# Sliding-window attention of a decoder trunk: heads interleaved in the small products, a tile's value product moved into a later unit, and the tail of the stage reordered

## The chip, the cores and the metric

One Trainium2 core runs the whole kernel. The metric is the device time of one execution in microseconds. 
## The reference

One inference step of a two-layer decoder over 512 prompt positions and 8 sample sequences of 8 positions each (576 columns, 1024 features). Layer 0 is half a SwiGLU, a state-space mixer, half a SwiGLU. Keys and values are projected once. Layer 1 is half a SwiGLU, the attention below, half a SwiGLU. Only the attention is touched here:

```python
def sink_alibi_attention(q, k, v, dist, valid, sinks):
    s = jnp.einsum('...qkgd,...skd->...kgqs', q, k).astype(jnp.float32) * (ATT_HEAD_DIM ** -0.5)
    s = s - alibi_slopes()[:, :, None, None] * dist
    s = jnp.where(valid, s, -jnp.inf)
    ...
    p = jax.nn.softmax(jnp.concatenate([s, sink_col], axis=-1), axis=-1)[..., :-1]
    return jnp.einsum('...kgqs,...skd->...qkgd', p.astype(v.dtype), v)
```

There are 16 query heads of 64 features on 4 key/value heads and a window of 128. A block of 128 prompt queries sees its own 128 keys and the 128 before. A sample sequence sees 128 cached keys and its own 8 new ones. The result goes through the output projection `o @ attn_w_o` and is added to the residual stream.

## The kernel before

The program is written engine by engine: five instruction lists (PE, ACT, DVE, POOL, SP) with hand-placed semaphore waits, each list run strictly in order. Nothing is scheduled by a planner.

**Weights.** They come in units of 128 output features by 1024 input features. SP loads a unit into `wraw` (two buffers), ACT rounds it to a high part (`split_hi`, L887 to L891), DVE subtracts to get the low part (`split_lo`, L1300 to L1303). A unit on PE (`unit`, L400; `half_unit`, L422) is 8 input tiles by three products (high weight with high and low data, low weight with high data) by two column halves of 288: 48 products. Unit n+2 can only be split when unit n has been multiplied, because they share a buffer.

**Attention loop.** `attention` of PE (L783) runs 8 units `j`; each yields the queries of two heads (`h` = 0 and 1, in partitions 0 to 63 and 64 to 127). For unit j the lists hold:

- PE (L786 to L799): the unit's 48 products; the 14 transposes of the probabilities of unit j-1 (`turn_probs`, L761); the scores of unit j, all of head 0, then all of head 1 (`scores`, L746, 8 matrix instructions a head); the value product of unit j-1, head 0, then head 1 (`weigh_values`, L772, 28 instructions).
- DVE (L1729 to L1743): queries out of PSUM (`qs`), `split_lo` of unit j+2, softmax input of both heads (`softmax_in`, four instructions a head), denominators, low part of the output of unit j-1 (`out_lo`).
- ACT (L1207 to L1227): `split_hi` of unit j+2, the sample queries (L1220), copies of the two transposed heads (`copy_probs`), exponentials of both heads, high part of the output of unit j-1 (`out_hi`).
- POOL (L1947): scales the probabilities of each head by the reciprocal denominators.

A matrix product of plain f32 operands is two matrix instructions in the trace; a transpose, and a product of the rounded (fp32r) operands, is one.

**Tail.** After the loop PE computes the sample scores (`sample_scores`, L810, 64 instructions of 136 columns), waits for the probabilities of unit 7, turns and weighs them, turns the sample probabilities (L827, L829), runs a quarter of the first two output tiles (`half_tile`, L835), then the sample values (L852 to L858): for each of 8 sequences and 2 pairs of heads one product with the cached values and one with the 8 new values, 64 instructions of 64 columns. The new values `Vnew` come back from HBM through a POOL DMA (L1957). The other three quarters of the two output tiles follow, and then `residual("o", ...)`, the remaining six output tiles.

## Time and profile before

| | |
|---|---|
| median of 3 runs | 2482.21 us (2475.89 to 2486.93) |
| profiled execution, its own time | 2485.29 us |
| its span, first to last instruction | 2483.7 us |
| mean granted TensorE clock | 0.986 |
| attention, first score product to the first product of the third output tile | 1845.8 to 2004.1 us |

The page gives each engine's busy time, forty slices of the span, and the chain of work that ended last. Times inside the span are counted from its start. "PEld" is TensorE's weight load, which runs beside the products. A PE that is busy need not be at its peak, because ends of products are modelled. The granted clock is given as a share of full speed (1.00 is 2.4 GHz, 0.50 is 1.2 GHz).

### The profile page before, as it was taken

The page shows a single profiled execution, that of the slowest core. Times are in us where ns is not written, and L with a number is a line of the kernel's source. Part 1 is how long each engine was busy: PE and PEld are TensorE (multiplying, and loading weights), DVE is VectorE, ACT ScalarE, POOL GpSimd, SP SyncE. Part 2 cuts the span into 40 slices and gives each one's busy share as a digit, 9 for nine tenths or more (in the row PEclk, how much of TensorE's full clock was granted, in tenths as well). Part 3 has the DMA queues.
Part 4 walks back from the last instruction along what each step waited for, and adds up shares of the span by engine and source line. Part 5 has one row for each costly group of instructions (what it writes and reads, how often), then busy time and mean ns, then how long its engine had stood idle before and what let it go on. Part 6 is the DMA issues. An engine that isn't in the chain of part 4 may idle for free.

```text
span 2483.7 us, 45807 instructions
## 1 busy us (share of the span) xinstructions
PE 2415.9 (97%) x18177; PEld 2365.4 (95%) x18177; DVE 1205.9 (49%) x1475; ACT 845.0 (34%) x1336; POOL 326.6 (13%) x278
## 2 busy tenths in 40 slices
PE   8999999899999999999999999999999999999997
PEld 8999999889888899999999999999989899999997
DVE  5344333778899934443433444343346354344323
ACT  4222222456666522222222322222235423222212
POOL 0000011322333221000012000000222140000021
PEclk9999999999999999999999999999999899999999
DMA  3222222335555322222222222222231022222222
GB/s 131 83 84 80 80 93 85 121 120 180 173 176 178 130 77 85 81 80 84 84 85 93 77 79 81 84 84 86 90 108 41 18 68 76 84 84 78 84 92 80
DMA packets 66239, 234.92 MB, mean 95 GB/s; under 512 B 7920, under 2 KB 8048, under 8 KB 66016
## 3 DMA queue, kind: packets, MB, share of 16 engines
q1 hardware_dynamic: 52560, 187.72, 22.3%
q0 software_dynamic: 8368, 31.59, 3.9%
q10 hardware_dynamic: 5248, 14.76, 1.8%
q8 instruction: 41, 0.67, 0.1%
q14 instruction: 22, 0.18, 0.0%
HBM read 221.37 MB, written 14.64 MB: 95 GB/s over the span
## 4 chain that ended last, share of the span: by engine, by line
PE 90%; DVE 5%; issue 2%; ACT 1%; DMA 1%; ACTq 0%; POOL 0%; DVEq 0%; POOLq 0%
PE psum L412 75%; PE psum L430 6%; DVE cacc L1418 1%; PE psum L757 1%; PE psum L707 1%; DVE wlo L1302 1%; PE psum L484 1%; DMA E<-decay_rows 1%; PE psum L768 1%; PE psum L603 1%; PE psum L598 1%; PE psum L780 1%; PE psum L840 0%; DVE grs L1654 0%; PE psum L633 0%
## 5 line engine op out<-in xcount | busy, mean ns | idle before, releaser
L1302 DVE TENSOR_TENSOR wlo<-wraw,whi 128x1024 fp32r<-128x1024 f32 x342 | 436.7, 1277 | 982.5 <-ACT whi L891 982.5
L891 ACT ACTIVATE whi<-wraw 128x1024 fp32r<-128x1024 f32 x349 | 369.4, 1059 | 946.8 <-PE psum L412 919.6
L412 PE MATMUL psum<-xhi,whi 128*128 128x288 f32 x3120 | 672.6, 297 | 11.4 <-POOL wlo L1969 7.3
L412 PE MATMUL psum<-xlo,whi 128*128 128x288 f32 x3120 | 669.5, 296 | 0.0
L412 PE MATMUL psum<-xhi,wlo 128*128 128x288 f32 x3120 | 669.5, 296 | 0.0
L412 PEld LDWEIGHTS psum<-xhi,whi 128*128 128x128 f32 x3120 | 504.7, 189 | 15.1 <-issue 14.4
L412 PEld LDWEIGHTS psum<-xlo,whi 128*128 128x128 f32 x3120 | 504.5, 189 | 0.0
L412 PEld LDWEIGHTS psum<-xhi,wlo 128*128 128x128 f32 x3120 | 504.3, 189 | 0.0
L412 PE MATMUL psum<-hhi,whi 128*128 128x288 f32 x1408 | 302.7, 296 | 0.0
L412 PE MATMUL psum<-hhi,wlo 128*128 128x288 f32 x1408 | 302.6, 296 | 0.0
L412 PE MATMUL psum<-hlo,whi 128*128 128x288 f32 x1408 | 302.6, 296 | 0.0
L412 PEld LDWEIGHTS psum<-hhi,wlo 128*128 128x128 f32 x1408 | 226.5, 189 | 0.0
L412 PEld LDWEIGHTS psum<-hhi,whi 128*128 128x128 f32 x1408 | 226.4, 189 | 0.0
L412 PEld LDWEIGHTS psum<-hlo,whi 128*128 128x128 f32 x1408 | 226.3, 189 | 0.0
L1823 POOL TENSOR_TENSOR sqsum<-x 128x576 f32<-128x576 f32 x6 | 6.9, 1146 | 1290.2 <-DVE x L1385 1232.8
L922 ACT ACTIVATE hhi<-hidden 128x576 f32 x87 | 59.7, 686 | 249.0 <-DVE hidden L1362 249.0
L1826 POOL TENSOR_TENSOR th<-x 128x576 f32 x41 | 72.5, 1769 | 463.5 <-DVE x L1385 387.8
L430 PE MATMUL psum<-xhi,whi 128*128 128x288 f32 x512 | 116.2, 308 | 3.8 <-DVE yall L1562 3.8
L919 ACT ACTIVATE silu<-gate 128x576 f32<-128x576 f32 x87 | 59.7, 686 | 174.4 <-DVE gate L1352 174.4
L430 PE MATMUL psum<-xhi,wlo 128*128 128x288 f32 x512 | 110.5, 298 | 0.0
L430 PE MATMUL psum<-xlo,whi 128*128 128x288 f32 x512 | 109.7, 296 | 0.0
L430 PEld LDWEIGHTS psum<-xhi,whi 128*128 128x128 f32 x512 | 81.8, 190 | 16.3 <-issue 15.0
(280 smaller groups left out, 2559.9 us busy)
## 6 DMA issues: line engine op xcount, KB each, us to landing
wraw<-w SPq DMA_DIRECT2D x349, 512.0 KB, 3.4
seg<-decay_rows ACTq DMA_DIRECT2D x16, 576.0 KB, 4.1
h0s<-ssm_state POOLq DMA_DIRECT2D x16, 512.0 KB, 5.6
h0T<-ssm_state_t POOLq DMA_DIRECT2D x16, 512.0 KB, 3.8
ssm_s<-h0s POOLq DMA_DIRECT2D x16, 512.0 KB, 3.5
E<-decay_rows ACTq DMA_DIRECT2D x32, 144.0 KB, 4.0
x<-x_in SPq DMA_DIRECT2D x8, 288.0 KB, 6.7
y<-ybuf SPq DMA_DIRECT2D x8, 288.0 KB, 2.4
```

What stands on the lines that cost most here:

```text
L412: last = pe.matmul(acc[:, 2 * pair + half, 0:HALF], wt[s][:, k * P:(k + 1) * P], m[:, k0 + k, half * HALF:(half + 1) * HALF], start=start ...
L430: last = pe.matmul(acc[:, 2 * pair + half, 0:HALF], wt[s][:, k * P:(k + 1) * P], m[:, k, half * HALF:(half + 1) * HALF], start=k == 0 and ...
L484: last = pe.matmul(acc[:, 2 * u + half, 0:HALF], wt[u][:, k * P:(k + 1) * P], mv[:, k, half * HALF:(half + 1) * HALF], start=k == 0 and i ...
L598: last = pe.matmul(bank[2][:, c * P:(c + 1) * P], xdd[:, c, :], Btm[:, g, c, :], start=True, stop=True)
L603: last = pe.matmul(bank[3 + b][:, :], xdd[seqs, NC, :], Bm[seqs, :, :], start=True, stop=True)
L707: last = pe.matmul(acc[:, 2 * d + half, 0:HALF], wt[s][:, at * P:(at + 1) * P], mv[:, k, half * HALF:(half + 1) * HALF], start=k == 0 and ...
L757: last = pe.matmul(psum[:, 2 + 2 * h + lo_col // 512, lo_col % 512:lo_col % 512 + (keys.stop - keys.start)], qs[rows, c * L:(c + 1) * L], ...
L891: act.activation(whi[n % 2][:], wraw[n % 2][:], ACT.Copy).then_inc(weights_hi, 1)
L919: act.activation(silu[:], gate[:], ACT.Silu).then_inc(silu_ready, 1)
L922: act.activation(hhi[:, i, :], hidden[:], ACT.Copy).then_inc(h_hi, 1)
L1302: dve.tensor_tensor(wlo[n % 2][:], wraw[n % 2][:], whi[n % 2][:].bitcast(F32), ALU.subtract).then_inc(weights_lo, 1)
L1826: pool.tensor_tensor(sq, x[:, k, :], x[:, k, :], ALU.mult).then_inc(squared, 1)
```

## The change

In the loop, PE's unit is cut in two halves; the value product of unit j-2 stands between them; then come the transposes of head 0 of unit j-1, the scores of unit j with the heads alternating, and the transposes of head 1. Both heads' transposes now use the same two PSUM banks. The value product alternates heads too. On DVE the order becomes: queries, denominator of head 1 of unit j-1, softmax input of both heads, denominator of head 0, `out_lo` of unit j-1, `split_lo` last. On ACT: copy of head 0, sample queries, copy of head 1, `split_hi`, exponentials, `out_hi`.

In the tail the sample scores are split into cached keys (64 instructions of 128 columns) and new keys (64 of 8 columns). The first output tile is computed as 512 prompt columns and 64 sample columns, in pieces, between the other steps; the second output tile's first half as well. The new values are no longer reloaded: a 0/1 mask of constants spreads the turned new probabilities block-diagonally over 8 sequences (`PTn`), and one 512-column product per pair of heads replaces 16 narrow ones. The order of work on unit 7 and the samples is changed on all three engines.

```diff
@@ PE
             def scores(j, kp):
...
+                for c in range(NC):
...
+                    for h in range(2):
+                        rows = slice(HD * h, HD * (h + 1))
                         last = pe.matmul(psum[:, 2 + 2 * h + lo_col // 512, lo_col % 512:lo_col % 512 + (keys.stop - keys.start)],
                                          qs[rows, c * L:(c + 1) * L], KVT[rows, kp, keys], start=True, stop=True)
...
             def weigh_values(j, kp):
                 pe.wait_ge(pt_ready, 2 * j + 2)
...
+                for c in range(NC):
+                    for b in ((c - 1, c) if c else (c,)):
+                        for h in range(2):
+                            v = slice((2 * kp + h) * HD, (2 * kp + h + 1) * HD)
+                            last = pe.matmul(bank[6][HD * h:HD * (h + 1), c * L:(c + 1) * L], VT[:, b, v], PT[:, h, c + b, :],
+                                             start=b == max(c - 1, 0), stop=b == c)
                 last.then_inc(pv_done, 1)
...
+                def body(g, kp):
 
                     j = 2 * g + kp
+                    pe.wait_ge(evicted, m + j + 2)
+                    half_unit(n + kp, 2 * g, 0, 0)
+                    if not (isinstance(j, int) and j == 1):
+                        weigh_values(j - 2, kp)
+                    half_unit(n + kp, 2 * g, 0, 1)
+                    turn_probs(j - 1, 0)
                     scores(j, kp)
+                    turn_probs(j - 1, 1)
...
                 sample_scores()
-                turn_probs(NK - 1)
-                weigh_values(NK - 1, 1)
+                weigh_values(NK - 2, 0)
...
             def sample_attention():
...
+                pe.wait_ge(ssoft, 2)
+                first_prompt(range(6))
+                turn_probs(NK - 1, 0)
+                first_prompt(range(6, 7))
+                second(0, range(7))
+                pe.wait_ge(sp_ready, 2)
+                for b in range(DEC_BATCH):
+                    pe.transpose(psum[:, 4 + b // 4, (b % 4) * P:(b % 4 + 1) * P], ssam[:, b, 0:WINDOW], ident)
+                pe.transpose(bank[1][0:S, 128:128 + P], pnew[:], ident).then_inc(sp_turned, 1)
+                turn_probs(NK - 1, 1)
+                weigh_values(NK - 1, 1)
+                pe.wait_ge(spt_ready, 2)
+                pe.wait_ge(vsam_loaded, 16)
                 pe.wait_ge(o_lo, NK)
...
+                for kp in range(2):
+                    v, rows = slice(kp * P, (kp + 1) * P), slice(64 * kp, 64 * kp + 64)
+                    pe.matmul(bank[6 + kp][:, :], kvsam[:, KVH * HD + kp * P:KVH * HD + (kp + 1) * P], PTn[:, :, rows],
+                              start=True, stop=False)
+                    for b in range(DEC_BATCH):
+                        last = pe.matmul(bank[6 + kp][:, b * 64:(b + 1) * 64], Vsam[:, b, v], PTs[:, b, rows], start=False,
+                                         stop=b == DEC_BATCH - 1)
                 last.then_inc(spv_done, 1)
+                first_prompt(range(7, 8))
+                second(0, range(7, 8))
+                first_samples()
+                second(1, range(NK), True)
@@ ACT
+                def body(g, kp):
+                    j = 2 * g + kp
+                    copy_probs(j - 1, 0)
+                    keep_queries(g, kp)
+                    copy_probs(j - 1, 1)
+                    split_hi(n + 2 + kp, 2 * g)
+                    exponentials(g, kp, 0)
+                    exponentials(g, kp, 1)
+                    out_hi(j - 1)
...
+                exponentials(g, kp, 0)
+                out_hi(j - 1)
                 sample_exponentials()
+                exponentials(g, kp, 1)
+                copy_probs(j, 0)
@@ DVE
+                def body(g, kp, first=False):
+                    j = 2 * g + kp
+                    queries(g, kp, first)
+                    if not first:
+                        denominator(j - 1, 1)
+                    softmax_in(g, kp, 0)
+                    softmax_in(g, kp, 1)
+                    denominator(j, 0)
                     if not first:
                         out_lo(j - 1)
+                    split_lo(n + 2 + kp, 2 * g)
...
+                queries(g, kp)
+                denominator(j - 1, 1)
+                split_lo(n + 2 + kp, 2 * g)
+                softmax_in(g, kp, 0)
                 sample_softmax()
+                denominator(j, 0)
+                softmax_in(g, kp, 1)
+                out_lo(j - 1)
+                sample_weights()
+                denominator(j, 1)
+                dve.wait_ge(sp_turned, 1)
+                dve.tensor_tensor(PTn[:], bank[1][0:S, 128:128 + P].unsqueeze(1).to_broadcast([S, DEC_BATCH, P]),
+                                  attc[0:S, OWN_SEQ:OWN_SEQ + DEC_BATCH].unsqueeze(2).to_broadcast([S, DEC_BATCH, P]),
+                                  ALU.mult).then_inc(spt_ready, 1)
+                out_lo(j)
@@ POOL
-                pool.wait_ge(units_done, PLAN["o"])
-                pool.dma_start(Vnew[:], kv_new_out[:, KVH * HD:].rearrange("(b t) v -> t b v", b=DEC_BATCH)).then_inc(vnew_loaded, 16)
```

Here `first_prompt(tiles)` is, for each input tile, three products of 512 columns; `second(half, tiles)` three of 288 columns; `first_samples()` is 24 products of 64 columns and waits for the low part of all sample outputs.

## Rows read from the trace of the kernel before

**Rows 1.** The page: the chain that ended last, shares of the span by engine.
```profile
PE 90%; DVE 5%; issue 2%; ACT 1%; DMA 1%; ACTq 0%; POOL 0%; DVEq 0%; POOLq 0%
```

**Rows 2.** Timeline, queries out of PSUM (DVE) of units 0, 1 and 7.
```profile
1844.91 0.76 DVE L1737 SCALAR_TENSOR_TENSOR qs<-psum,rstd 128x576 f32<-128x576 f32 x1
...
1858.81 0.76 DVE L1737 SCALAR_TENSOR_TENSOR qs<-psum,rstd 128x576 f32<-128x576 f32 x1 [1.44 <-PE psum L412]
...
1945.76 0.76 DVE L1737 SCALAR_TENSOR_TENSOR qs<-psum,rstd 128x576 f32<-128x576 f32 x1 [1.81 <-PE psum L412]
```

**Rows 3.** Timeline of unit 4: start, us, engine line op out<-in xcount [idle before <-releaser].
```profile
1899.45 0.58 ACT L1205 ACTIVATE ohi<-psum 128x512 f32 x1
1900.20 0.69 DVE L1726 TENSOR_TENSOR olo<-psum,ohi 128x512 f32 x1 [0.24 <-ACT ohi L1205]
1901.98 1.69 PE L768 MATMUL psum<-cst,probs 128*128 128x128 f32 x14
1902.36 0.76 DVE L1737 SCALAR_TENSOR_TENSOR qs<-psum,rstd 128x576 f32<-128x576 f32 x1 [1.47 <-PE psum L412]
1903.27 1.23 DVE L1302 TENSOR_TENSOR wlo<-wraw,whi 128x1024 fp32r<-128x1024 f32 x1 [0.16 <-ACT whi L891]
1903.60 3.61 PE L757 MATMUL psum<-KVT,qs 64*128 64x128 f32 x16
1905.55 1.01 DVE L1704 SCALAR_TENSOR_TENSOR sc<-attc,psum 128x768 f32<-128x768 f32 x1 [1.05 <-PE psum L757]
1907.14 0.19 PEld L780 LDWEIGHTS psum<-PT,VT 128*64 128x64 f32 x2 [0.33 <-issue]
1908.46 1.01 DVE L1704 SCALAR_TENSOR_TENSOR sc<-attc,psum 128x768 f32<-128x768 f32 x1
1909.96 0.30 PEld L412 LDWEIGHTS psum<-xhi,whi 128*128 128x128 f32 x2 [0.17 <-issue]
```

**Rows 4.** The chain that ended last, in order of time: one unit's 48 products.
```profile
1910.03 6.59 PE psum L412 x48
```

**Rows 5.** Timeline of the mixer: products that alternate row groups (L603) or heads (L633).
```profile
736.14 1.13 PE L603 MATMUL psum<-Bm,xdd 32*128 32x512 f32 x4
...
745.43 1.09 PE L633 MATMUL psum<-E,xdt 128*64 128x128 f32 x16
```

**Rows 6.** Windows: length, busy us (instructions) of PE, PEld, DVE, ACT, POOL, granted clock, DMA.
```profile
1845.80:1850.50 4.70, 4.68 (x16) 3.60 (x16) 2.29 (x4) 1.70 (x3) 1.79 (x4) 0.50 0.89 340
1895.56:1910.03 14.47, 14.43 (x108) 13.13 (x107) 9.03 (x17) 8.18 (x26) 3.79 (x2) 1.00 0.11 36
...
1958.60:1962.90 4.30, 3.24 (x15) 2.87 (x15) 2.75 (x5) 1.91 (x3) 1.55 (x2) 0.50 0.05 15
...
1974.10:1991.60 17.50, 17.50 (x66) 14.16 (x64) 0.00 (x0) 0.00 (x0) 0.00 (x0) 0.58 0.00 0
1991.60:2001.00 9.40, 9.40 (x52) 9.38 (x52) 1.79 (x5) 1.62 (x5) 0.00 (x0) 0.69 0.01 2
```

**Rows 7.** Timeline of the tail, same columns as rows 3.
```profile
1953.36 2.06 PE L818 MATMUL psum<-Ksam,Qsam 64*32 64x136 f32 x64
...
1958.65 3.22 PE L768 MATMUL psum<-cst,probs 128*128 128x128 f32 x14 [3.23 <-DVE olo L1726]
...
1959.87 1.29 DVE L1762 TENSOR_REDUCE snmax<-ssam 128x8 f32<-128x1088 f32 x1
...
1961.91 0.92 ACT L1187 ACTIVATE PT<-psum 128x896 f32<-128x896 f32 x1 [0.58 <-PE psum L768]
...
1971.11 1.02 ACT L1247 ACTIVATE PTs<-psum 128x1024 f32<-128x1024 f32 x1 [2.85 <-PE psum L829]
...
1991.73 1.59 ACT L1256 ACTIVATE ohi<-psum 64x256 fp32r<-64x256 f32 x4 [18.65 <-PE psum L857]
...
1993.35 1.78 DVE L1778 TENSOR_TENSOR olo<-psum,ohi 64x256 fp32r<-64x256 f32 x4 [24.36 <-ACT ohi L1256]
...
2004.09 0.53 PE L412 MATMUL psum<-ohi,whi 128*128 128x288 f32 x2
```

More of the change, by code:

```diff
@@ new lines, in turn_probs @@
+            def turn_probs(j, h):
+                pe.wait_ge(p_ready, 2 * j + h + 1)
+                if h == 0 and not (isinstance(j, int) and j == 0):
+                    pe.wait_ge(o_lo, j)
+                if h == 1:
+                    pe.wait_ge(pt_ready, 2 * j + 1)
+                for t in range(2 * NC - 1):
+                    last = pe.transpose(psum[:, 6 + t // 4, (t % 4) * P:(t % 4 + 1) * P], probs[:, h, (t + 1) * P:(t + 2) * P], ident)
+                last.then_inc(p_turned, 1)
@@ L846, in sample_attention @@
-                pe.wait_ge(evicted, TILE["o"] + 2)
-                half_tile(0, 0)
-                pe.wait_ge(spt_ready, 3)
-                pe.wait_ge(vsam_loaded, 16)
-                pe.wait_ge(vnew_loaded, 16)
-                for b in range(DEC_BATCH):
-                    for kp in range(2):
-                        out = bank[3 + kp][:, b * 64:(b + 1) * 64]
-                        v, rows = slice(kp * P, (kp + 1) * P), slice(64 * kp, 64 * kp + 64)
-                        pe.matmul(out, Vsam[:, b, v], PTs[:, b, rows], start=True, stop=False)
-                        last = pe.matmul(out, Vnew[:, b, v], PTn[:, b, rows], start=False, stop=True)
+                n = PLAN["o"]
@@ new lines, in o_tiles @@
+                def o_tiles(d, out, cols, tiles, done=False):
+                    s = (n + d) % 2
+                    pe.wait_ge(weights_lo, n + d + 1)
+                    for k in tiles:
+                        if cols.start < SEQ:
+                            pe.wait_ge(o_lo, k + 1)
+                        if cols.stop > SEQ:
+                            pe.wait_ge(os_lo, 4)
+                        for i, (wt, src) in enumerate(((whi, ohi), (whi, olo), (wlo, ohi))):
+                            last = pe.matmul(out, wt[s][:, k * P:(k + 1) * P], src[:, k, cols],
+                                             start=k == 0 and i == 0, stop=k == NK - 1 and i == 2)
+                    if done:
+                        last.then_inc(units_done, 1)
@@ L875, in _ @@
             sample_attention()
-            residual("o", [NK], ohi, olo, o_lo, 4, done=1)
+            residual("o", [NK], ohi, olo, o_lo, 0, done=1)
             gate_up("gu3")
@@ L1180, in attention, with copy_probs @@
                 n, m = PLAN["q"], TILE["q"]
[L1182 to L1185 removed]
+                def copy_probs(j, h):
+                    act.wait_ge(p_turned, 2 * j + h + 1)
+                    if not (isinstance(j, int) and j == 0):
                         act.wait_ge(pv_done, j)
[L1187 to L1189 removed]
@@ new lines, in exponentials @@
+                def exponentials(g, kp, h):
+                    hh = 4 * g + 2 * kp + h
+                    act.wait_ge(soft, 4 * hh + 4)
+                    for c in range(NC):
+                        act.activation(probs[:, h, 2 * L * c:2 * L * (c + 1)], sc[:, h, 2 * L * c:2 * L * (c + 1)],
+                                       ACT.Exp, bias=nmax[:, h, c:c + 1],
+                                       accum_out=rsum[:, h, c:c + 1]).then_inc(p_exp, 1)
+                    head = g + 8 * kp + 4 * h
+                    act.activation(esink[:, h, :], nmax[:, h, :], ACT.Exp,
+                                   bias=acol(SINK, head)).then_inc(p_exp, 1)
```

278 lines of the change are left out of this document (116 added, 162 removed).

## The prediction

> **What bounds the kernel now.** I read first the chain that ended last: PE holds 90% of it [rows 1], so over the whole span PE's own list is the bound, and time saved anywhere else counts only where PE waits. Only the stretch from 1845.8 to 2004.1 us is touched, so I read the timeline there. From the queries of unit 1 to those of unit 7, six periods take 1945.76 - 1858.81 = 86.95 us [rows 2], 14.49 each. In such a period PE is busy for 14.43 us of 14.47, at full clock [rows 6]: the loop is bound by PE. But the second engine is close. DVE starts `qs` of unit 4 at 1902.36 after 1.47 us of idleness, so its last work before, `out_lo`, ended at 1900.89 [rows 3]. One period earlier, at 1887.87, it had started `qs` of unit 3. Its round, from queries over scores, both softmaxes, exponentials, `out_hi` to `out_lo`, is thus 13.0 us long: only 1.5 us below PE's. The tail is different: PE waits 3.23 us for `olo` before it can turn unit 7 [rows 7], then runs at half clock (0.50 [rows 6]). It spends 17.5 us on the 64 narrow sample-value products, at a mean clock of 0.58 [rows 6], and is still at 0.69 after them.
>
> **The sum, part by part** (against the profiled execution's own 2485.29 us, which is 3.1 above the median of the runs shown).
>
> *Scores with heads alternating.* The 16 instructions take 3.61 us, one head after the other [rows 3]. The heads lie in different rows of the array. No score product alternates before, but L603 in the mixer does so with row groups: four instructions of 512 columns in 1.13 us [rows 5]. At the scores' rate (3584 columns in 3.61 us, 1.0 ns a column) they would take 2.05, so overlapping leaves 0.55 of the time. Bounds are 1.8 (perfect) and 3.6 (none); I take 2.0.
>
> *Values with heads alternating.* 28 instructions, from 1907.14 to 1909.96, 2.82 us [rows 3]. L633 has the same shape (128 rows, 64 columns of weights, 128 columns moved) and already alternates: 16 in 1.09, or 0.068 each [rows 5]. So 1.9, bounds 1.8 and 2.8. The Trainium skill (TensorE: Matmul & The Clock Gate, Part 3, The mechanism) says that a weight load overlaps with running products only when its row group differs, and here both heads use all rows. By that rule the value product stays at 2.8, PE again bounds the loop near 14.4 and the sum below would be some 3 us smaller; L633's row does not bear it out.
>
> *The loop.* PE's list falls to 6.59 [rows 4] + 14 transposes at 0.12 (1.69 for 14 [rows 3]) + 2.0 + 1.9 = 12.2, with one more change of shape (0.17 to 0.33 of idleness at each [rows 3]) about 12.9. But DVE's round gets longer. `split_lo`, 1.23 us, stood in DVE's wait for the scores, with 1.05 of idleness still behind it [rows 3]; moved to the end it stands in the round. The softmax starts a little sooner: before, the scores waited for all 14 transposes and began 1.24 after `qs`; now they wait for `qs` alone (0.9), and 2.0 later the first head is free, 2.9 instead of 3.19. The new round is 13.0 + 1.23 - 0.3 = 13.95. Now DVE bounds, PE waits about a microsecond for `qs` in every unit, and most of the saved PE time is not seen: 6 x 0.54 = 3.2 us. POOL's 1.9 us per head [rows 6] now stands between `qs` and the second head's transposes; it ends about 3.2 after `qs`, when the scores end, and costs PE 0.4 that DVE's round hides. If ACT's `split_hi`, now ahead of the exponentials, came late, it would delay these; it ends about 6.4 after `qs`, the first softmax (2.91 a head, 1905.55 to 1908.46 [rows 3]) at 5.8 and the second at 8.7, and the latter decides.
>
> *The start.* The scores of unit 0 ran 4.70 us at half clock [rows 6]. Times 0.55 that is 2.1 off. The unit after them starts earlier in the slow stretch and gives part back: I take 1.4 (bounds 0 and 2.1).
>
> *The tail*, counted from `qs` of unit 7 at 1945.76 [rows 2]. It ended with the third output tile at 2004.09 [rows 7], 58.3 later. Now PE has: scores to 2.9, transposes to 4.3, 64 sample scores at 0.032 (2.06 for 64 [rows 7]) to 6.3, the 64 of 8 columns to 8.3. No row shows such short ones: 0.032 is the nearest row, nothing and 0.068 (L633) the bounds, 0 to 4.4 us. Values of unit 6 to 10.2. Filler of 18 x 512 columns at 6.59/48 x 512/288 = 0.24: to 14.6. It then waits for `out_lo` of unit 6. DVE reaches that after `split_lo` (2.4), softmax of head 0 (5.8), an idle wait for the sample scores (8.3), sample adds, maximum (1.29 [rows 7]; the adds alike) and negation 3.1, a denominator, softmax of head 1 (2.9), `out_lo`: 15.5. With half a microsecond for a slower clock the transposes end at 17.1. More filler (3 x 0.24 and 21 x 0.137) to 20.7, 17 transposes to 22.5. ACT copies `PTs` (1.02) and `PT` (0.92) [rows 7], 23.8; values of unit 7 to 25.7; `out_hi` and `out_lo` with handoffs 1.7, 27.4.
>
> Then the sample values: four wide instructions and 32 narrow ones instead of 64 narrow. At full clock 4 x 0.5 + 32 x 0.12 (as a transpose, the nearest row with 128 columns of weights) = 5.8. At half clock the wide ones cost 0.67 each (4.70 us for 3584 columns, unit 0) and the narrow ones 0.23 (14 transposes in 3.24) to 0.27 (64 in 17.5) [rows 6]: 10.7. A mean of 0.58 over 17.5 us says that the clock fell about 2.8 us into the same narrow work, though PE was busy throughout. Before it there are now waits of 1.3 and 1.7 us too. I take a fall soon after the start, 9.5: to 36.9. High and low parts of the sample outputs follow as before, 1991.73 to 1995.13 = 3.4 [rows 7], and only then may the 24 sample products of the first tile run: 40.5. They are narrow and at half clock, 24 x 0.23, 46.0. The second tile's second half, 24 of 288 columns at 0.24 (the rate that a mean clock of 0.69 gives for the stretch behind the values [rows 6]): 51.8. Gain 58.3 - 51.8 = 6.5. The `Vnew` reload hid before and saves nothing; the extra PSUM reads of the first tile lie beside PE.
>
> Sum: 1.4 + 3.2 + 6.5 = 11.1 us, so 2474.2 for the profiled execution and 2471 beside the median. Behind 2004 the work is PE-bound and unchanged, so what is gained stays.
>
> **The rivals.** *The clock holds through the tail* (19 us). The stretch of filler is dense, and the values are half as many. With 5.8 for the values, 24 x 0.13 for the sample products and 3.3 for the last 24, the tail ends at 43.4, gain 14.9, together 19.5: 2463. Against it: the clock fell inside this very kind of product before.
>
> *The scores do not overlap.* Then the softmax starts 4.3 after `qs`, the round is 15.35, the loop loses 5.2, the start gains nothing, the tail 5: no change, 2482. L603's row speaks against it, but with 32 rows a group, not 64.
>
> *The clock falls inside the loop.* This is the one that ends slower. Place: the wait between the first transposes and the scores, which did not exist. Before, PE was busy for 14.43 of 14.47 us; now it is idle 1 to 1.5 us a unit, beside transposes. If each unit ran 8 us at half clock, PE's 12.9 would become 16.9 and the loop would lose 6 x 2.4 = 14.5; with the start and tail gains 6.6 slower, 2489. Half clock throughout would double the 12.9 and cost some 65. It decides once half-clock time passes 2 x (14.49 - 12.9) = 3.2 us a unit. Against it: in the old loop the clock stood at 1.00 although scores and values left half the array empty.
>
> **Numbers.** Forecast 0.53, clock held 0.22, no overlap 0.13, clock falling in the loop 0.12. A measurement of this kernel can tell 0.5%, 12.4 us, from no change. The forecast's own range, with the unknown prices, is 2464 to 2479; a third of it lies below 2469.8. So faster 0.53 x 0.35 + 0.22 = 0.40; slower only if the clock falls for most of the loop, 0.07; same 0.53. The range for 8 in 10 takes in the clock held and no overlap: 2459 to 2484.
>
> **What would show it.** Right: periods of `qs` near 13.9, DVE no longer idle ahead of `qs` while PE waits for `qs` ahead of the scores; 16 scores in 2.0 and 28 values in 1.9; half clock in the windows of the sample values and of the sample products of the first tile. Wrong: periods at 12.9 (DVE's round is shorter than I make it) or above 14.5, a clock below 1.00 in the loop, or a tail whose clock stays at 1.00.

## The result, and the profile after

The changed kernel takes 2465.78 us (median of 4 runs, 2464.5 to 2469.73), the kernel before, run beside it, 2481.89. The ratio is 0.9933 [0.9915, 0.9951]: 16.1 us faster, or 0.67%. The profiled execution took 2464.5 us, its span 2462.9, its mean granted clock 0.989. Of the five executions of a later run, e13, one took 6823.58 us; it is left out of that run's ratio.

The stretch that the change touches is compared from the first `qs` to the third output tile, because work ahead of it, which the change leaves alone, ended 2.1 us earlier in this profile than in that of before. Before, the stretch took 2004.09 - 1844.91 = 159.18 us [rows 2, 7]; now 1983.38 - 1842.82 = 140.56. It shrank by 18.6.

The page of the changed kernel: the chain that ended last, by engine (rows 1 had PE at 90% and "issue" at 2%). PE's share fell by 4 points and that of "issue" rose by 3. In the attention loop this chain now follows POOL's list, scaling after scaling, and the time between them is "issue", for which the view names no releaser. So the page does not say what bounds the loop; the timeline has to.

```profile
PE 86%; DVE 5%; issue 5%; ACT 1%; POOL 1%; DMA 1%; ACTq 0%; DVEq 0%; POOLq 0%
```

The timeline of the changed kernel, `qs` of units 0, 1, 2 and 7, which answers to rows 2. From unit 2 to unit 7 five periods take 65.73 us, 13.15 each (before 72.36, 14.47 each).

```profile
1842.82 0.76 DVE L1766 SCALAR_TENSOR_TENSOR qs<-psum,rstd 128x576 f32<-128x576 f32 x1
1853.83 0.75 DVE L1766 SCALAR_TENSOR_TENSOR qs<-psum,rstd 128x576 f32<-128x576 f32 x1
1869.69 0.75 DVE L1766 SCALAR_TENSOR_TENSOR qs<-psum,rstd 128x576 f32<-128x576 f32 x1
...
1935.42 0.75 DVE L1766 SCALAR_TENSOR_TENSOR qs<-psum,rstd 128x576 f32<-128x576 f32 x1
```

One unit of the changed kernel, same columns as rows 3.

```profile
1882.98 0.75 DVE L1766 SCALAR_TENSOR_TENSOR qs<-psum,rstd 128x576 f32<-128x576 f32 x1
1883.79 1.79 PE L753 MATMUL psum<-KVT,qs 64*128 64x128 f32 x16 [0.75 <-DVE qs L1766]
1884.10 1.89 POOL L2009 TENSOR_TENSOR probs<-probs,rden 128x1024 f32<-128x1024 f32 x1 [3.47 <-DVE rden L1753]
1885.73 1.01 DVE L1735 SCALAR_TENSOR_TENSOR sc<-attc,psum 128x768 f32<-128x768 f32 x1 [1.71 <-PE psum L753]
1886.04 0.98 PE L766 MATMUL psum<-cst,probs 128*128 128x128 f32 x7 [0.47 <-POOL probs L2009]
1890.14 1.75 PE L775 MATMUL psum<-PT,VT 128*64 128x128 f32 x28
1894.50 0.69 DVE L1757 TENSOR_TENSOR olo<-psum,ohi 128x512 f32 x1 [2.59 <-ACT ohi L1218]
1895.10 1.22 DVE L1331 TENSOR_TENSOR wlo<-wraw,whi 128x1024 fp32r<-128x1024 f32 x1
1896.24 0.75 DVE L1766 SCALAR_TENSOR_TENSOR qs<-psum,rstd 128x576 f32<-128x576 f32 x1
```

Read it from the end: `olo`, `wlo` and `qs` follow each other, and the last two have no bracket, so DVE does not wait ahead of `qs` any more. (It waits 2.59 us ahead of `olo`, for ACT's `out_hi`: the round that bounds the loop runs over DVE and ACT.) PE waits now, 0.75 us for `qs` ahead of the scores, and 0.47 for POOL ahead of the second transposes. The 16 scores take 1.79 us (3.61 before), the 28 value products 1.75 (2.82 before).

The tail of the changed kernel answers to rows 7.

```profile
1936.37 1.20 DVE L1331 TENSOR_TENSOR wlo<-wraw,whi 128x1024 fp32r<-128x1024 f32 x1
1936.53 2.78 POOL L2009 TENSOR_TENSOR probs<-probs,rden 128x1024 f32<-128x1024 f32 x1 [3.16 <-DVE rden L1753]
...
1939.37 0.98 PE L766 MATMUL psum<-cst,probs 128*128 128x128 f32 x7 [1.35 <-POOL probs L2009]
...
1942.05 0.72 PE L820 MATMUL psum<-Ksam,Qsam 64*32 64x8 f32 x64
...
1949.46 0.95 PE L766 MATMUL psum<-cst,probs 128*128 128x128 f32 x7 [0.64 <-DVE olo L1757]
...
1956.82 1.75 PE L775 MATMUL psum<-PT,VT 128*64 128x128 f32 x28 [1.16 <-ACT PT L1276]
1960.08 1.09 PE L868 MATMUL psum<-PTn,kvsam 64*128 64x512 f32 x2 [1.51 <-DVE olo L1757]
1961.10 2.08 PE L871 MATMUL psum<-PTs,Vsam 128*128 128x64 f32 x16
1963.11 2.07 PE L868 MATMUL psum<-PTn,kvsam 64*128 64x512 f32 x2
1965.11 3.67 PE L871 MATMUL psum<-PTs,Vsam 128*128 128x64 f32 x16
...
1972.37 0.39 PE L838 MATMUL psum<-ohi,whi 128*128 128x64 f32 x1 [1.48 <-DVE olo L1836]
...
1983.38 0.43 PE L410 MATMUL psum<-ohi,whi 128*128 128x288 f32 x2
```

In unit 7 the change has `split_lo` right behind `qs`, and POOL's scaling, which starts 0.16 us behind it, takes 2.78 us instead of 1.89; PE waits 1.35 for it. (e3, below, has the same in its loop.)

The sample values take 8.46 us, from 1960.08 to 1968.54, against 17.5 before. Their second half is the slower one: 2.07 for two 512-column instructions that took 1.09, and 3.67 for 16 narrow ones that took 2.08. The windows of the changed kernel (columns as in rows 6) say why: the first is a unit of the loop at clock 1.00, then the clock goes to 0.50 some 2.9 us into the sample values and stays there to the end of the tail.

```profile
1895.50:1908.80 13.30, 12.00 (x108) 10.73 (x108) 8.46 (x16) 8.19 (x24) 3.79 (x2) 1.00 0.12 39
1960.00:1963.00 3.00, 2.92 (x18) 2.19 (x18) 0.00 (x0) 0.00 (x0) 0.00 (x0) 0.98 0.02 5
1963.00:1983.40 20.40, 18.93 (x74) 16.70 (x74) 4.64 (x7) 3.35 (x6) 1.15 (x1) 0.50 0.06 19
```

### The profile page after: what moved, and what is told of

It reads as the page before. It is cut to its first block, busy times and chain, and to the rows that moved or that the text cites. A ratio compares the mean times of both kernels' runs of the same rounds, so it can differ in the third digit from the quotient of the medians.

```text
span 2462.9 us, 45809 instructions
## 1 busy us (share of the span) xinstructions
PE 2387.5 (97%) x18206; PEld 2338.2 (95%) x18206; DVE 1205.2 (49%) x1477; ACT 844.2 (34%) x1334; POOL 326.7 (13%) x277
## 4 chain that ended last, share of the span: by engine, by line
PE 86%; DVE 5%; issue 5%; ACT 1%; POOL 1%; DMA 1%; ACTq 0%; DVEq 0%; POOLq 0%
PE psum L410 74%; PE psum L428 6%; DVE cacc L1450 1%; PE psum L705 1%; POOL probs L2009 1%; DVE wlo L1331 1%; PE psum L838 1%; PE psum L482 1%; PE psum L596 1%; PE psum L601 1%; DVE grs L1686 0%; PE psum L631 0%; DMA E<-decay_rows 0%; ACT whi L906 0%; PE psum L623 0%
## 5 line engine op out<-in xcount | busy, mean ns | idle before, releaser
L410 PEld LDWEIGHTS psum<-xhi,wlo 128*128 128x128 f32 x3008 | 486.3, 189 | 0.0
L410 PEld LDWEIGHTS psum<-xlo,whi 128*128 128x128 f32 x3008 | 486.2, 189 | 0.0
```

The costliest lines, as they stand in the source:

```text
L410: last = pe.matmul(acc[:, 2 * pair + half, 0:HALF], wt[s][:, k * P:(k + 1) * P], m[:, k0 + k, half * HALF:(half + 1) * HALF], start=start ...
```

## Experiments

Every run was timed against the kernel before. As the work ahead of the attention starts it at another time in each execution (the first `qs` lies between 1837.5 and 1849.7), the table also gives the profiled execution's times from the first `qs` to that of unit 7, and from there to the third output tile.

| run | median us | ratio to before | units 2 to 7, one period | first `qs` to unit 7 | tail | both |
|---|---|---|---|---|---|---|
| before | | | 14.47 | 100.85 | 58.33 | 159.18 |
| changed | 2465.78 | 0.9933 [0.9915, 0.9951] | 13.15 | 92.60 | 47.96 | 140.56 |
| e1 | 2466.82 | 0.9930 [0.9906, 0.9955] | 13.19 | 92.70 | 48.05 | 140.75 |
| e2 | 2469.41 | 0.9941 [0.9918, 0.9964] | 13.58 | 94.05 | 48.53 | 142.58 |
| e3 | 2465.34 | 0.9920 [0.9893, 0.9948] | 13.29 | 90.88 | 47.97 | 138.85 |
| e4 | 2487.68 | 1.0013 [1.0001, 1.0025] | 14.61 | 101.78 | 60.99 | 162.77 |
| e5 | 2470.35 | 0.9931 [0.9914, 0.9948] | 13.53 | 93.76 | 52.58 | 146.34 |
| e6 | 2461.72 | 0.9898 [0.9880, 0.9916] | 13.14 | 91.42 | 44.31 | 135.73 |
| e7 | 2468.18 | 0.9930 [0.9904, 0.9956] | 13.14 | 91.42 | 52.92 | 144.34 |
| e9 | 2459.34 | 0.9898 [0.9881, 0.9914] | 12.36 | 86.01 | 41.99 | 128.00 |
| e10 | 2471.05 | 0.9948 [0.9932, 0.9965] | 14.42 | 100.76 | 43.48 | 144.24 |
| e11 | 2443.72 | 0.9829 [0.9808, 0.9850] | 11.94 | 84.08 | 36.04 | 120.12 |
| e12 | 2457.76 | 0.9887 [0.9871, 0.9904] | 13.15 | 91.44 | 43.23 | 134.67 |
| e13 | 2475.07 | 0.9958 [0.9942, 0.9974] | 13.14 | 91.45 | 56.04 | 147.49 |

Four runs have the changed kernel's loop untouched (e6, e7, e12, e13): 91.4 us to unit 7 in each, 1.2 less than in the profile of the changed kernel itself, all of it in the first two units (25.7 for 26.9). In that profile PE waited 2.12 us for POOL in unit 1, and the clock then fell (two rows and a window below): the scores of unit 1 take 2.99 us instead of 1.79. The four runs wait 0.91 to 2.02 us at the same place and keep 1.00 there. Differences below about 1.2 us in that column mean nothing.

```profile
1855.71 0.99 PE L766 MATMUL psum<-cst,probs 128*128 128x128 f32 x7 [2.12 <-POOL probs L2009]
1856.63 2.99 PE L753 MATMUL psum<-KVT,qs 64*128 64x128 f32 x16
...
1857.00:1861.00 4.00, 4.00 (x25) 3.03 (x22) 1.32 (x3) 1.05 (x3) 0.86 (x1) 0.57 0.00 0
```

**e1: one head's scores after the other.**

```diff
@@ PE, scores
-                for c in range(NC):
...
-                    for h in range(2):
-                        rows = slice(HD * h, HD * (h + 1))
+                for h in range(2):
+                    rows = slice(HD * h, HD * (h + 1))
+                    for c in range(NC):
```

> The changed kernel with the scores of head 0 all before those of head 1 again. Theory (the loop is bound by a round over DVE and ACT, and the alternation helps only because it lets the second head's transposes, its copy and ACT's weight split come earlier): the softmax of head 0 starts as soon after the queries as now (2.7 us), the second transposes come 1.7 later, the exponentials of head 0 start near 7.4 us after the queries instead of 6.0, and the period of the queries goes from 13.26 to about 14.3; 8 to 9 us slower than the changed kernel. Rival 1 (the rival of the prediction, the softmax has to wait for both heads): softmax of head 0 4.3 us after the queries, period above 15, 14 us slower. Rival 2 (PE time is not seen at all): period stays at 13.3, at most 3 us slower from start and tail.

The scores take longer, as these rows of e1 show, and the sum stays: 140.75 us against 140.56. The 8 to 9 us of the theory did not come; rival 2 is what happened.

```profile
1897.95 2.55 PE L753 MATMUL psum<-KVT,qs 64*128 64x128 f32 x16 [0.75 <-DVE qs L1766]
1900.43 0.98 PE L766 MATMUL psum<-cst,probs 128*128 128x128 f32 x7
```

The softmax of head 0 starts 2.76 us after `qs`, as in the changed kernel (2.75): it waits for its own head only, which now comes first. The longer scores fill PE's wait for POOL ahead of the second transposes: the second row has no bracket, where the changed kernel has 0.47. The scores' alternation thus gives nothing in this loop.

Nor is it what takes most of the 1.82 us off the scores. In e1 the order within the scores is that of the kernel before, and they take 2.55 us, not 3.61. The kernel before makes head 1's scores wait for ACT's copies of the last unit's transposes (`pt_ready`); its chain shows the two heads apart, and the second starts just when the copies end, 1905.37 (two rows of the chain, then one of the timeline):

```profile
1903.67 1.71 PE psum L757 x8
1905.43 1.78 PE psum L757 x8
1903.68 1.69 ACT L1187 ACTIVATE PT<-psum 128x896 f32<-128x896 f32 x2
```

The change moved that wait away from between the heads. In e1, where nothing stands between them, head 1's first product starts 0.77 us behind head 0's, while head 0's are still running. So 1.06 of the 1.82 us came without any alternation, by these rows with the wait's going, and 0.76 with it.

**e2: one head's values after the other.**

```diff
@@ PE, weigh_values
-                for c in range(NC):
-                    for b in ((c - 1, c) if c else (c,)):
-                        for h in range(2):
+                for h in range(2):
...
+                    for c in range(NC):
+                        for b in ((c - 1, c) if c else (c,)):
```

> The changed kernel with the value products of head 0 all before those of head 1 again (28 instructions: 2.8 us instead of 1.75). Theory (PE has about 0.7 us of slack in a unit): the period goes from 13.26 to about 13.6, 3 to 5 us slower with the two value products of the tail. Rival (PE bounds the loop): 1.07 a unit in full, 8 to 9 us slower.

```profile
1906.00 2.89 PE L775 MATMUL psum<-PT,VT 128*64 128x128 f32 x28
```

The value products of e2 take 2.89 us for 1.75; 0.4 a period of these 1.14 are seen, since PE had 0.75 to spare ahead of the scores (0.26 is left). The period of 13.65 is the theory's; the stretch is 2.0 us longer and the median 3.6, where 3 to 5 were expected.

**e4: the kernel before, with both alternations and no other order.**

```diff
@@ kernel before, PE: scores and weigh_values
-                    if h == 1:
-                        pe.wait_ge(pt_ready, 2 * j)
+                pe.wait_ge(pt_ready, 2 * j)
+                for c in range(NC):
...
+                    for h in range(2):
```

> The kernel before with nothing but the heads alternating in scores and value products; since head 1's scores share PSUM banks with its transposes, all scores now wait for both copies. Theory (alternation alone gains nothing in the loop, the new order of work is what lets it count): scores start 1.8 us later, period 14.5 to 14.9 instead of 14.49; start and tail gain 3 to 5; in all 0 to 4 us faster than before. Rival (the shorter products themselves carry the gain): period 12 to 13, 10 us or more faster than before.

```profile
1895.90 1.93 PE L768 MATMUL psum<-cst,probs 128*128 128x128 f32 x14 [1.86 <-DVE olo L1725]
1898.84 1.79 PE L756 MATMUL psum<-KVT,qs 64*128 64x128 f32 x16 [1.01 <-ACT PT L1186]
1900.56 1.75 PE L778 MATMUL psum<-PT,VT 128*64 128x128 f32 x28
```

The same 1.79 and 1.75 us, 2.9 us of products less a unit, and no gain: all of it turns into waits, 1.86 for `olo` and 1.01 for the copy of the transposes. (The second wait is this edit's own: all scores now share a wait that only head 1 had.) The 0 to 4 us that were expected did not come either; the tail is 2.7 us longer. So alternation frees PE, and only the new order of the lists (values a unit later, transposes on either side of the scores) makes it count.

**e5: the values back behind the second transposes.**

```diff
                     half_unit(n + kp, 2 * g, 0, 0)
-                    if not (isinstance(j, int) and j == 1):
-                        weigh_values(j - 2, kp)
                     half_unit(n + kp, 2 * g, 0, 1)
...
                     turn_probs(j - 1, 1)
+                    weigh_values(j - 1, 1 - kp)
```

> The changed kernel with the value product of a unit's predecessor taken straight behind the second head's transposes (as the kernel before had it), instead of one unit later between the two halves of a unit. Theory (the later place is a part of the gain, because PE no longer waits for ACT's copy of the second head): in the changed kernel PE is busy 12.0 of 13.3 us a unit, and the copy of the second head ends about 1.1 us after its transposes. Put back, PE waits those 1.1 us in each unit: periods of 14.1, about 4 to 6 us slower over six of them. Rival (the round of DVE from qs to qs sets the period and PE has 1.3 us to spare, which pays for the wait; the values come earlier, and so do out_hi and out_lo): periods of 13.0 to 13.3, between 2 us faster and the same time.

The wait was there, 1.01 us for ACT's copy, but the steady period was 13.6, not 14.1: the wait for `qs` shrank from 0.75 to 0.26. The loop lost 1.2 to 2.3 us. Another 4.6 were lost in the tail, where the values of unit 6 no longer fill the time ahead of the sample softmax; PE waited 0.71 and 1.48 us there and the first output tile began at half clock. The total, 5.8, is of the theory's size, but most of it came by another way.

**e3: the weight split early.** ACT's `split_hi` first in the unit, DVE's `split_lo` behind `qs` and the denominator.

```diff
@@ ACT body
+                    split_hi(n + 2 + kp, 2 * g)
                     copy_probs(j - 1, 0)
...
@@ DVE body
                         denominator(j - 1, 1)
+                    split_lo(n + 2 + kp, 2 * g)
                     softmax_in(g, kp, 0)
```

> The changed kernel with the weight split back at the head of the round: split_hi first on ACT, split_lo on DVE in its wait for the scores. Theory (DVE's round with split_lo at its end bounds at 13.26, and right below it stands the path queries, denominator, POOL's scaling, second transposes, unit, queries, worth about 13.0): period near 13.0, 1 to 2 us faster. Rival (only DVE's round bounds): 12.1, 7 us faster. A third reading (split_lo at the end costs nothing): no change.

DVE became idle ahead of `qs`, 0.85 us, but the period was 13.42, and the median did not change (1 to 2 us less was expected): a new path took its place. In this timeline of e3 POOL's scaling takes 2.82 us instead of 1.89, and PE waits 1.40 for it.

```profile
1897.66 0.76 DVE L1766 SCALAR_TENSOR_TENSOR qs<-psum,rstd 128x576 f32<-128x576 f32 x1 [0.85 <-PE psum L428]
1898.63 1.23 DVE L1331 TENSOR_TENSOR wlo<-wraw,whi 128x1024 fp32r<-128x1024 f32 x1
1898.78 2.82 POOL L2009 TENSOR_TENSOR probs<-probs,rden 128x1024 f32<-128x1024 f32 x1 [3.28 <-DVE rden L1753]
1901.66 0.98 PE L766 MATMUL psum<-cst,probs 128*128 128x128 f32 x7 [1.40 <-POOL probs L2009]
```

**e10 and e9: the second denominator early** (in the loop, and so in unit 7 too), in e10 alone, in e9 with the edit of e3.

```diff
@@ DVE body
-                    if not first:
-                        denominator(j - 1, 1)
...
                     denominator(j, 0)
+                    denominator(j, 1)
```

> The changed kernel with only one edit in the loop: the denominator of the second head stands right behind that of the first, ahead of out_lo, instead of behind the next qs; the weight splits stay where the change has them. Theory (in the changed kernel the period of 13.26 is DVE's own list from qs to qs, in which split_lo's 1.2 us has no cover, so POOL's place matters nothing): POOL scales the second head before qs and the second transposes stop waiting, but qs comes no sooner: periods 13.2 to 13.6, no change. Rival (POOL's late scaling is what holds the loop): periods near the 12.43 that this edit gave together with the early split.

> The changed kernel with ACT's split_hi first in its unit and DVE's split_lo behind qs (as in the run with the early split, whose period was 13.42), and the denominator of the second head computed right behind that of the first, ahead of out_lo, instead of behind the next qs. Theory (with the early split the period is set by a circle: qs, denominator, POOL's scaling of the second head, the second transposes, the unit, qs; the denominator's place closes it): POOL scales the second head before qs, PE no longer waits for it, DVE is idle ahead of qs and PE becomes the bound again at its busy 12.0 to 12.6 us: 4 to 6 us faster over six periods. Rival (POOL's scaling now runs beside more of DVE's work, takes longer, and the second transposes or the first head's wait as before): periods stay at 13.2 to 13.4, no change.

e10 was worse than either theory, periods of 14.2 and one of 15.55. Its timeline shows POOL unharmed and now DVE's split held up, 2.20 us for 1.22, right ahead of `qs`: the 0.98 that the period is longer. PE then waits 1.7 us for `qs` in each unit. In the unit of 15.55 the clock fell behind that wait (the window 1910.50 to 1913.00 has 0.50), and the scores took 3.09 us:

```profile
1906.14 1.89 POOL L2007 TENSOR_TENSOR probs<-probs,rden 128x1024 f32<-128x1024 f32 x1 [0.45 <-DVE rden L1753]
1906.92 2.20 DVE L1331 TENSOR_TENSOR wlo<-wraw,whi 128x1024 fp32r<-128x1024 f32 x1
1909.84 3.09 PE L753 MATMUL psum<-KVT,qs 64*128 64x128 f32 x16 [1.74 <-DVE qs L1766]
```

In e9 the split has the slack behind `qs` (it takes 1.45 us there), and POOL is through before it matters: PE no longer waits for `qs` or POOL, only 0.6 for `olo`, and the period is 12.36, as the theory had it. Its tail is 6.0 us shorter too: the wait of 1.35 us for POOL is gone, and the sample values run at full clock (5.8 us).

**e12: sample values of the second pair first**, whose PSUM bank is free, so that nothing waits for `olo` of unit 7 there.

```diff
-                pe.wait_ge(o_lo, NK)
-                for kp in range(2):
+                for kp in (1, 0):
+                    if kp == 0:
+                        pe.wait_ge(o_lo, NK)
```

> The changed kernel with only this: the sample values of the second pair of heads are computed first. Their PSUM bank is free, so PE no longer waits 1.51 us for out_lo of unit 7 right ahead of them. Nothing else moves. Theory (this wait, right ahead of the narrow products, is what brings the clock down 3 us later): the clock stays at 1.00 through the sample values, 6 us instead of 8.5, and the tail is 1.5 + 2.5 = 4 us faster at least. Rival (the waits further back, of 1.35 and 1.16 us, count too, or the narrow products do it alone): the clock falls in the sample values again, and only the 1.5 us of the wait are gained, or less.

One wait of 1.51 us away, 4.7 us gained in the tail. The windows of e12 show the sample values at full clock, 5.9 us, and the fall only behind the next wait (2.45 us, ahead of the second window). The row of that wait stands first.

```profile
1973.82 0.39 PE L838 MATMUL psum<-ohi,whi 128*128 128x64 f32 x1 [2.45 <-DVE olo L1837]
```

```profile
1964.20:1970.10 5.90, 5.90 (x39) 4.32 (x37) 0.69 (x1) 0.60 (x1) 0.00 (x0) 1.00 0.01 3
1973.80:1979.00 5.20, 5.18 (x25) 5.20 (x25) 0.00 (x0) 0.00 (x0) 0.00 (x0) 0.50 0.00 0
```

**e6 and e7: the seven filler tiles** of the second output tile's first half moved, in e6 into the two waits ahead of the sample values, in e7 among the narrow products.

```diff
@@ e6
-                second(0, range(7))
...
                 turn_probs(NK - 1, 1)
+                second(0, range(3))
                 weigh_values(NK - 1, 1)
+                second(0, range(3, 7))
```

```diff
@@ e7, behind each narrow product of the sample values
-                second(0, range(7))
...
+                        k = 4 * kp + b // 2
+                        if b % 2 == 0 and k < 7:
+                            second(0, range(k, k + 1))
```

> The changed kernel with the seven tiles of the second output tile's first half moved: three of them in front of the values of unit 7, where PE waited 1.16 us, and four between them and the sample values, where it waited 1.51. Theory (the narrow products of the sample values bring the clock down by themselves, as the fall came 2.9 us into them with PE busy): the clock falls to 0.50 again about 3 us into the sample values; the waits are filled, but so is less of the time ahead of the sample transposes, where PE then waits: between 2 us faster and the same. Rival (the waits ahead of the sample values bring the clock down): the clock stays at 1.00 through the sample values and behind; values 6 us instead of 8.5, sample products 3 instead of 5.1, the second tile's 24 products 3.3 instead of 6: 6 to 9 us faster.

> The changed kernel with the same seven filler tiles (three products of 288 columns each) spread among the 32 narrow products of the sample values, one tile behind every second sequence. Theory (narrow products bring the clock down): mixed with wide ones they do not, the clock stays at 1.00 longer, and the tail is 0 to 6 us faster although PE waits longer ahead of the sample transposes. Rival (waits bring it down): without the filler ahead of the sample transposes PE idles there, the clock falls there or sooner than in the changed kernel, and the tail is 3 to 6 us slower.

In e6 the sample values ran at full clock and the sample products behind them, after a wait of 2.44, at half: 3.65 us gained, less than the rival's 6 to 9. Of the rival's terms only the sample values came (5.8 us); the sample products took 5.1 us and the last 24 products 5.6, at half clock or nearly, and a wait of 1.51 opened ahead of the second transposes of unit 7. In e7, with that wait and the others (1.50, 1.01, 1.51), the fall came earlier than in the changed kernel, some 1 us into the sample values, and the tail is 5.0 us longer, as the rival had it. Mixing the narrow products with wide ones did not hold the clock there; as this run adds waits too, it does not show what mixing does alone. First the window of e6, then that of e7:

```profile
1961.90:1967.80 5.90, 5.90 (x38) 4.32 (x37) 0.00 (x0) 0.00 (x0) 0.00 (x0) 1.00 0.01 3
```

```profile
1959.60:1974.50 14.90, 14.88 (x57) 12.52 (x58) 0.00 (x0) 0.00 (x0) 0.00 (x0) 0.54 0.00 1
```

**e13: the block-diagonal product taken apart** into 16 products of 64 columns, each next to its product with the cached values, as in the kernel before.

```diff
-                    pe.matmul(bank[6 + kp][:, :], kvsam[:, KVH * HD + kp * P:KVH * HD + (kp + 1) * P], PTn[:, :, rows],
-                              start=True, stop=False)
                     for b in range(DEC_BATCH):
+                        out = bank[6 + kp][:, b * 64:(b + 1) * 64]
+                        pe.matmul(out, kvsam[:, KVH * HD + kp * P:KVH * HD + (kp + 1) * P], PTn[:, b, rows],
+                                  start=True, stop=False)
```

> The changed kernel with the block-diagonal product of the new sample values taken apart: for each of 8 sequences and 2 pairs of heads one product of 64 columns with the 8 new values' block, next to the one with the cached values, as the kernel before ordered them; 64 narrow instructions instead of 32 narrow and 4 of 512 columns. Theory (a narrow instruction costs 0.125 us at full and 0.215 at half clock whatever it multiplies, a 512-column one 0.5 and 1.0): 64 narrow ones cost 8.0 at full and 13.8 at half clock; with the clock falling 3 us in as before, about 24 at full and 40 at half clock, 11.6 us instead of 8.5, so the tail is about 3 us slower. Rival (the wide ones are no cheaper, as they are plain f32 over 512 columns): 8.5 to 9 us, no difference.

```profile
1960.60:1978.50 17.90, 17.89 (x65) 14.60 (x66) 0.00 (x0) 0.00 (x0) 0.00 (x0) 0.57 0.00 1
```

The sample values of e13 take 17.7 us (1960.62 to 1978.35) at a mean clock of 0.57: what they took before (17.5 at 0.58 [rows 6]). My 11.6 was a miss, since I priced each narrow one at 0.125 and 0.215; where weights of 64 and of 128 rows take turns, a pair of instructions costs 0.36 at full and 0.62 at half clock. The block-diagonal form is worth some 9.3 us in the sample values and 8.1 in the tail, the largest part of the change that one run took out.

**e11: together**, the loop of e9 with `out_hi` between the exponentials of the two heads and `out_lo` ahead of the second denominator; in the tail the order of e12, sample outputs taken pair by pair, and three filler tiles moved into waits.

```diff
@@ ACT body
                     exponentials(g, kp, 0)
+                    out_hi(j - 1)
                     exponentials(g, kp, 1)
-                    out_hi(j - 1)
@@ ACT, sample outputs (DVE alike with os_hi)
-                act.wait_ge(spv_done, 1)
-                for kp in range(2):
+                for kp in (1, 0):
+                    act.wait_ge(spv_done, 2 - kp)
```

> The run with the early split and the early denominator (period 12.43, 128.0 us from the first qs to the third output tile), with out_hi between the exponentials of the two heads and out_lo right behind the first head's denominator (PE waited 0.6 us in each unit for out_lo), and in the tail: sample values of the second pair of heads first, whose bank is free, so that out_hi and out_lo of unit 7 lie beside them; sample outputs taken pair by pair; two filler tiles behind the last transposes and one more behind the sample values. Theory: the waits of 0.6 a unit go, periods 11.9 to 12.1 (3 us over six); in the tail 1.5 of wait ahead of the sample values, 0.8 ahead of the values of unit 7 and 1 to 1.5 ahead of the sample products go, 3 to 4 us, and the clock holds longer or as long: 121 to 123 us in all, 6 us faster than that run. Rival (the round of DVE and ACT over softmax and exponentials is the bound by now, and out_hi delays the second head's exponentials): periods stay at 12.4, and only the tail's 3 us are seen.

It beats both kernels: 2443.72 us, 41 below the kernel before beside it and 22 below the changed one by the medians (26 by the ratios). Its period of 11.94 and its 120.1 us in all are the theory's, or a little better; as it changes several things at once, it does not show what each gave. The tail gained more than expected, because full clock lasts through the sample values and the sample products. First a row of its tail, then two windows: no wait above 0.64 is left in the tail, and the clock still falls, behind the 24 narrow sample products.

```profile
1955.20 0.27 PE L838 MATMUL psum<-ohi,whi 128*128 128x64 f32 x1 [0.34 <-DVE olo L1836]
```

```profile
1955.20:1957.80 2.60, 2.60 (x24) 2.60 (x24) 0.00 (x0) 0.00 (x0) 0.00 (x0) 1.00 0.00 0
1957.80:1961.00 3.20, 3.20 (x16) 3.20 (x16) 2.66 (x3) 1.83 (x2) 1.15 (x1) 0.52 0.00 0
```

## Why the prediction was right, and where not

The time lay in the range (2459 to 2484), 5 us below the forecast of 2471, and the gain was 0.67%: just past the 0.5% that I had called measurable, a case to which I had given 0.40, less than the 0.53 for no change. The forecast's mechanism held in the loop (DVE's round becomes the bound, most of PE's saving is not seen) and in the tail (the fall of the clock); its sizes were too small. It summed to 11.1 us; the stretch gained 18.6 in the profiled execution: 1.6 in units 0 to 2, 6.6 in the five periods behind them and 10.4 in the tail.

- **DVE becomes the bound of the loop: right, with its round too long.** The term was 6 x 0.54 = 3.2 us, from a round of 13.95. Measured is 13.26, and five periods gained 6.6 us where the term gives 2.7. The failed step is "`out_lo`, ended at 1900.89", 13.0 us behind `qs` of unit 3. I read one unit, and it was the longest: in the others from unit 1 to unit 6 `out_lo` ends 12.3 to 12.8 behind `qs`. In the next unit, in the timeline of the kernel before, `out_lo` starts 11.96 us behind `qs` (1902.36) and ends after 12.65:

```profile
1914.32 0.69 DVE L1726 TENSOR_TENSOR olo<-psum,ohi 128x512 f32 x1 [0.25 <-ACT ohi L1205]
```

  That is 0.35 of the 0.69. The softmax started 2.75 behind `qs`, 0.44 sooner and not 0.3: another 0.14. And DVE's instructions overlap at their ends: `wlo` starts 0.60 behind `olo` and `qs` 1.14 behind `wlo`, while I had added their full 0.69 and 1.23: 0.18.
- **The start and the first period: about right, in part by luck.** 1.4 + 0.54 was forecast for units 0 to 2; it is 1.6 in the profile (28.49 to 26.87) and 2.8 in the four runs with the same loop. In the profile the first period is 2.9 us shorter and the second 1.3 longer, with the wait and the fall of the clock in unit 1, which the forecast did not have.
- **The prices of the products: right as numbers, the scores' not for the reason given.** Scores 1.79 (2.0 taken, bounds 1.8 and 3.6), values 1.75 (1.9 taken). The mixer's row carried the values' (e2). I put the scores' whole 3.61 down to their order; by e1 the alternation is worth 0.76 of the 1.82, and the rest is the wait for ACT's copies that stood between the heads, which I had not read. The working for values at 2.8 was wrong too: PE's 12.9 and 0.9 more are 13.8, not 14.4, still below DVE's 13.95, so the sum would not have changed by 3 us; e2, with values at 2.89, has periods of 13.65. The Trainium skill's rule (TensorE: Matmul & The Clock Gate, Part 3, The mechanism), that a weight load overlaps only when the row group differs, does not agree with e2: with all 128 rows in use, the same 28 instructions take 2.89 us one head at a time and 1.75 with the heads' columns taking turns.
- **The rival "the scores do not overlap" did not happen.** The alternated scores take 1.79 us. Its price, 15.35 a round, stays untested: it supposed alternated scores that do not overlap, so that the softmax waits for both heads. e1 is another case: its scores stand head by head and still overlap in part (2.55), and the softmax, which waits for head 0 alone, starts no later.
- **The tail: right in kind, 6.5 forecast, 10.4 measured.** By its own waypoints behind `qs` of unit 7: the short sample scores end at 7.3 instead of 8.3, since 64 of 8 columns take 0.65 us to the next instruction's start, not 2.0 (I took the price of 136 columns), and in spite of PE's wait of 1.35 for POOL, which the forecast did not have; the transposes of unit 7, which wait for `olo`, end at 14.8 instead of 17.1, 1.0 from the same cause, some 0.6 from DVE's steps (6.6 us from the sample scores to the end of `out_lo` for 7.2), and most of the rest from the half microsecond that I had laid in for a slower clock (it was 1.00 there); the sample values take 8.46 and not 9.5; the sample products start at 36.95 instead of 40.5.
- **The clock in the tail: right.** It fell soon after the start of the sample values and stayed at 0.50 to 1983. The reason given, that such narrow products bring it down "though PE was busy throughout", is half of it. e12 takes one wait away and the values run through at full clock; e9 and e10 keep this wait, but not that of 1.35 us for POOL near the start of the tail, and run through too, though e10 waits 1.88 us for `qs` shortly before that place; e11 falls behind narrow products with hardly a wait. So waits ahead of the narrow work count (e12), the fall can come behind narrow work with short waits (e11), and how the two add up was not settled.
- **The clock in the loop: right from unit 2 on.** It stayed at 1.00 in units that leave PE idle for 1.3 us of 13.3, and the rival that ended slower did not happen. But its mechanism is real: the clock fell for some 3 us in unit 1 of the changed kernel's profile, behind a wait of 2.12 us, and in one unit of e10, behind one of 1.74. Each cost that unit 1.2 to 1.3 us in the scores.
- **What the term "costs PE 0.4 that DVE's round hides" missed:** POOL's place behind `qs`. It is hidden only while DVE's round is the longer one. In e3, where it is not, it sets the period, 13.42, with 0.93 of that from POOL's scaling being held up by the split. DVE's round (13.26) was the bound of the change, but neither freeing it alone (e3) nor POOL's place alone (e10) gained anything in the loop; the two together did (e9, 12.36, and e11).

## What to carry to other kernels

When a change frees the engine that bounds a loop, measure the next engine's round over several units and from start to start of its instructions, not from one unit and by durations: here that was 0.5 us of 0.7. Saved time counts only where the lists are reordered around it (e4 gained nothing from the same products). Narrow work with a wait ahead of it costs twice where the clock falls: let it use what is free first (e12: 1.5 us of wait, 4.7 us gained), and merge narrow products with a mask where the data allow it (e13).

## What the runs showed of the hardware that I had not expected

- DVE's weight split and POOL's scaling hold each other up. Whichever starts second waits: POOL started 0.15 us behind the split in e3 and took 2.82 us for 1.89, the split started 0.78 behind POOL in e10 and took 2.20 for 1.22; in unit 7 of the changed kernel POOL started 0.16 behind the split and took 2.78. DVE's `olo`, which reads PSUM, ran beside POOL in e10 at its usual 0.69. The Trainium skill has this rule (SBUF — State Buffer, SBUF: two separate sides: the port pair that both engines share is "an exclusive lock, not a bandwidth split", taken by a DVE operation with two SBUF inputs while GpSimd reads SBUF), and these rows agree; it bears on where `split_lo` may stand, and I had not used it.
- Products of 8 columns cost 0.010 us each (64 in 0.65, to the next instruction's start), a third of the 0.032 of those with 136 columns [rows 7].
- Products of 64 columns cost 0.125 us each at full clock where all weights have 128 rows (16 in 2.00, e12) but 0.18 where weights of 64 and 128 rows take turns (e13).
